# A two-layer diffusion backbone: a new plan for where the expert groups go in, and the unit ends on ScalarE's queue

## The reference, cut to what matters

```python
hl = modulate(rmsnorm(xl, norm1_g[l]), ...)           # norm1
out_c, out_l = token_mixers(hc, hl, w_in[l], ...)     # attention (da), mLSTM (ml), short convolution; merge
xl = xl + g1 * out_l
hl = modulate(rmsnorm(xl, norm2_g[l]), ...)
xl = xl + g2 * peer(hl, wq, keys, u_tab, v_tab)       # experts
```

## The kernel before

| stage | segment 1 | segment 2 | segment 5 |
|---|---|---|---|
| first route (pair 1) | 42, of which 22 at its last step | - | 40, of which 20 at its last step |
| swap | 2 | 2 | - |
| q | 3 | 4 | 3 |
| da, its 8 steps + 1 | 6 + 1 | 12 + 1 | 10 + 1 |
| ml_on (2 steps) | - | 5 | 4 |
| mc (8 steps) | 12 | 14 | 12 |
| mln (1 step) | 1 | 2 | 1 |
| merge (30 steps) | 35 | 40 | 33 |
| last route (8 steps) | 42 | 48 | 40 |

## Time and profile before

### The profile page before, as it was taken

How to read it: one execution, slowest core, us unless ns; L and a number is a source line. 1 busy time by engine, 2 the same in 40 slices (tenths; PEclk the granted TensorE clock), 3 DMA queues, 4 the chain that set the end, 5 groups by cost and what they waited for, 6 DMA issues and landing times.

```text
span 6141.9 us, 65028 instructions
## 1 busy us (share of the span) xinstructions
PE 3690.8 (60%) x22376; PEld 2569.9 (42%) x22376; DVE 2908.5 (47%) x6866; ACT 1680.3 (27%) x4742; POOL 1387.8 (23%) x1297
## 2 busy tenths in 40 slices
PE   4888786337774357774445566878545787433333
PEld 2677575215552235553223344767422565211111
DVE  0212324745447754446745444331575444764444
ACT  0111201214432242442233222210123343222222
POOL 0000000232222222232333333000122222223433
PEclk7798687658886677887666687759766788665555
DMA  7333034798998888998889998204578799789998
GB/s 285 137 129 126 1 110 168 302 351 337 359 380 313 312 315 317 350 408 313 336 350 386 369 404 369 100 1 146 195 289 339 278 376 387 308 307 379 405 410 361
DMA packets 331978, 1767.03 MB, mean 288 GB/s; under 512 B 96672, under 2 KB 109824, under 8 KB 140416
## 3 DMA queue, kind: packets, MB, share of 16 engines
q0 software_dynamic: 184320, 1342.26, 54.8%
q1 hardware_dynamic: 139648, 399.64, 17.9%
q10 hardware_dynamic: 7680, 20.98, 1.2%
HBM read 1737.95 MB, written 24.68 MB: 287 GB/s over the span
## 4 chain that ended last, share of the span: by engine, by line
PE 35%; DMA 26%; DVE 16%; ACT 5%; DVEq 4%; issue 4%; POOL 2%; ACTq 2%; SPq 0%; PEld 0%; PEldq 0%; POOLq 0%
PE psum L474 24%; DMA arena<-in_uv,arena 22%; PE psum L825 5%; DVE arena L2135 5%; POOL arena L1187 2%; DVE arena L2037 1%; DVE arena L2030 1%; DVE arena L2031 1%; PE psum L434 1%; DMA arena<-in_w_mix 1%; DVEq L2137 1%; DMA arena<-in_norm_g 1%; PE psum L655 1%; DMA arena<-x_rows 1%; PE psum L656 1%
## 5 line engine op out<-in xcount | busy, mean ns | idle before, releaser
L1187 POOL DMA_INDIRECT arena<-in_uv,arena x1280 | 1383.5, 1081 | 4719.6 <-PE psum L825 2741.5
L2135 DVE CUSTOM_DVE_ANT_0 arena<-arena 128x1024 f32<-128x1024 f32 x1280 | 1554.4, 1227 | 1418.7 <-DMA arena<-in_uv,arena 1329.5
L474 PE MATMUL psum<-arena 128*128 128x256 f32 (+2 forms) x8608 | 2041.3, 397 | 144.4 <-DVEq L1571 53.5
L825 PE MATMUL psum<-arena 128*32 128x256 f32 x10240 | 988.2, 523 | 1719.7 <-ACTq L1552 1657.3
L474 PEld LDWEIGHTS psum<-arena 128*128 128x128 f32 (+1 forms) x8608 | 1696.0, 203 | 514.3 <-issue 92.7
L825 PEld LDWEIGHTS psum<-arena 128*32 128x32 f32 x10240 | 335.1, 137 | 2288.9 <-ACTq L1552 1855.7
L1544 ACT ACTIVATE arena<-arena 128x2 f32<-128x2 f32 x640 | 131.1, 205 | 1879.6 <-DVEq L2137 1652.4
L1551 ACT ACTIVATE arena<-arena 128x32 f32<-128x32 f32 x1280 | 341.8, 314 | 45.6 <-issue 1.4
L434 PE MATMUL psum<-arena 128*128 128x128 f32 (+1 forms) x680 | 136.3, 361 | 340.5 <-DVE arena L1630 78.7
L1548 ACT ACTIVATE arena<-arena 128x1 f32<-128x1 f32 x1280 | 307.8, 287 | 46.7 <-issue 2.6
L434 PEld LDWEIGHTS psum<-arena 128*128 128x128 f32 (+1 forms) x680 | 105.2, 188 | 382.5 <-issue 191.7
(11 more groups left out here) (210 smaller groups left out, 2829.5 us busy)
## 6 DMA issues: line engine op xcount, KB each, us to landing
arena<-in_w_in SPq DMA_DIRECT2D x116, 1024.0 KB, 6.8
arena<-in_w_mix SPq DMA_DIRECT2D x120, 768.0 KB, 8.4
arena<-in_w_ada SPq DMA_DIRECT2D x32, 1536.0 KB, 16.2
arena<-in_w_wq SPq DMA_DIRECT2D x40, 1152.0 KB, 5.3
arena<-in_w_wo SPq DMA_DIRECT2D x20, 1024.0 KB, 9.2
arena<-h_rows ACTq DMA_DIRECT2D x160, 128.0 KB, 7.4
arena<-in_uv,arena POOLq DMA_INDIRECT x1280, 12.5
arena<-ada_rows SPq DMA_DIRECT2D x15, 512.0 KB, 8.0
```

The source lines that it names most:

```text
L474: ins = mm(out, a, b, start=(i == 0), stop=(i == last))
L825: ins = mm(acc_bank(u)[32 * q:32 * q + 32, gg * 256:gg * 256 + 256], DIAG[:, c, :], RING[:, sl, D + q * 256:D + (q + 1) * 256], start=(h, ...
L1187: pool.indirect_dma_start(RING[:, sl, :], None, io["uv"], bass.IndirectOffsetOnAxis(PICKED_U[b][:, h_, tg, a:a + 1], 0)).then_inc(gathered ...
L2135: V_.tensor_tensor_reduce(out=RING[:, sl, 0:D], in0=RING[:, sl, 0:D], in1=XT[:, gg, :], scale=1.0, scalar=0.0, op0=ALU.mult, op1=ALU.add, ...
```

## The change

Three edits. **The costs** in `steps()` are replaced: no longer microseconds of a step but roughly the number of groups that go beside it. **The sharing out** in `quotas()` gives a step the fraction cost/left of the places still to be given, so that places held back by `routed_upto` are spread over the steps after it; and segments 1 and 5 get 12 places more (`more` 16 to 28), segment 3 and the tail 12 fewer. **The unit ends**: SP's `group` is empty; the loads of G2P and XP and the stores of XP are issued by ACT, one place later in the walk than before, the stores after ACT has waited for `added`.

The plan after:

| stage | segment 1 | segment 2 | segment 5 |
|---|---|---|---|
| first route (pair 1) | 27, of which 7 at its last step | - | 26, of which 6 at its last step |
| swap | 1 | 1 | - |
| q | 3 | 2 | 2 |
| da, its 8 steps + 1 | 18 + 5 | 24 + 4 | 25 + 4 |
| ml_on | - | 12 | 12 |
| mc | 9 | 8 | 8 |
| mln | 10 | 8 | 8 |
| merge | 29 | 24 | 25 |
| last route | 54 | 45 | 46 |

Segment 3: norm1 14, kv 6, mlp 11, ml 23, norm1 14, qkv 9, mlp 16, mc 11 (four empty). In the last route of segments 1, 2 and 5 `routed_upto` now holds some places back too: the last steps of segment 2 and 5 are 5, 4, 8.

```diff
@@ -86,26 +86,26 @@
 
     n = len(pairs)
     if kind == "norm1":
-        return [4.0] * (2 * n)
+        return [5.0] * (2 * n)
     if kind in ("qkv", "kv", "q"):
-        return [2.5 if op[0] == "turn" else 7.0 for op in qkv_ops(kind) for p in pairs]
+        return [0.9 if op[0] == "turn" else 0.7 for op in qkv_ops(kind) for p in pairs]
     if kind == "da":
-        return [6.0 if u[2] > CT else 3.0 for u in da_units(l, pairs)] + [5.0] * n
+        return [3.1 if u[2] > CT else 2.0 for u in da_units(l, pairs)] + [4.0] * n
     if kind == "mlp":
-        return [1.0] * n + [3.5] * (len(ml_blocks(l, pairs)) * n) + [7.0] * (2 * n) + [6.0]
+        return [0.7] * n + [0.8] * (len(ml_blocks(l, pairs)) * n) + [1.0] * (2 * n) + [2.0]
     if kind in ("ml", "ml_back", "ml_on"):
-        return [10.0] * len(ml_units(kind, l, pairs))
+        return [6.0 if u[5] else 4.0 for u in ml_units(kind, l, pairs)]
     if kind == "mc":
-        return [7.0] * (2 * n) + [7.0] * (6 * n)
+        return [1.0] * (8 * n)
     if kind == "edge":
-        return [6.0] * 4
+        return [0.9] * 4
     if kind == "mln":
-        return [5.0] * n
+        return [8.0] * n
     if kind == "merge":
-        return [5.2] * 24 + [7.0] * 4 + [4.0] * 2
+        return [0.74] * 24 + [1.0] * 4 + [1.6] * 2
     if kind == "route":
-        return [24.0] * PH
-    return [8.0]
+        return [5.8] * PH
+    return [1.0]
 
 
 UNITS = [(0, t, f) for t in (2, 3, 0, 1, 4, 5) for f in range(2)] + [(1, t, f) for t in range(CT, NT) for f in range(2)]
@@ -136,7 +136,7 @@
     c = [("swap", 0, (2,))] + second_pair(0)
     c2 = [(k, 1, (0,)) for k in ("norm1", "kv", "mlp", "ml")] + ahead
     e1 = [("route", 1, (1,))] + second_pair(1)
-    tile, more = 2 * GROUPS, 16
+    tile, more = 2 * GROUPS, 28
     p0, p1 = sequence(range(0, 12)), sequence(range(12, 20))
     b_end, c_end, e_end = 2 * tile + more, 4 * tile + more, 2 * tile + more
     return [(a, [], 0), (b, p0[:b_end], 0), (c, p0[b_end:c_end], 0), (c2, p0[c_end:], 0), (first_pair(1), [], 0), (e1, p1[:e_end], 0),
@@ -162,15 +162,16 @@
 
     out = []
     for stages, items, lead in SEGMENTS:
-        total = sum(sum(steps(*st)) for st in stages)
-        done, cum, rows = lead, 0.0, []
+        left = sum(sum(steps(*st)) for st in stages)
+        done, aim, rows = lead, float(lead), []
         for st in stages:
             row = []
             for n, cost in enumerate(steps(*st)):
-                cum += cost
-                want = lead + int(round((len(items) - lead) * cum / total))
+                aim += (len(items) - aim) * min(1.0, cost / left)
+                left = max(left - cost, 1e-6)
                 if st[0] == "route" and n < PH - 1:
-                    want = max(done, min(want, routed_upto(items, st[1], st[2], n - 1)))
+                    aim = min(aim, float(routed_upto(items, st[1], st[2], n - 1)))
+                want = max(done, int(round(aim)))
                 row.append(want - done)
                 done = want
             rows.append(row)
@@ -398,6 +399,10 @@
 
             _, t, f = UNITS[u]
             return route_of(u) % 2, h, 4 * (t % 2) + 2 * f + gg
+
+        def ada_row(l, p, j):
+            st = 0 if p == 0 else 1
+            return ada_rows[2 * l + 1 - st:2 * l + 2 - st, j * D:(j + 1) * D]
 
         def last_unit(l, t):
             return UNITS.index((l, t, 1))
@@ -1028,10 +1033,6 @@
                     yield
                 barrier()
 
-            def ada_row(l, p, j):
-                st = 0 if p == 0 else 1
-                return ada_rows[2 * l + 1 - st:2 * l + 2 - st, j * D:(j + 1) * D]
-
             def merge(kind, l, pairs):
                 (p,) = pairs
                 g1, xs, mods = buf(l, p, "G1", [D]), buf(l, p, "XS2", [2, D]), buf(l, p, "MT", [2, D])
@@ -1090,28 +1091,7 @@
                 barrier()
 
             def group(i):
-                item = PSEQ[i]
-                if item is not None:
-                    u, g = item
-                    l, t, f = UNITS[u]
-                    if g == 8:
-                        if new_stream(u):
-                            if u:
-                                sp.wait_ge(s("added"), u)
-                            row = ada_row(l, t // 2, 5)
-                            for q in range(4):
-                                for gg in range(2):
-                                    sp.dma_start(G2P[32 * q:32 * q + 32, gg * 256:gg * 256 + 256], row[:, q * 256:(q + 1) * 256].to_broadcast([32, 256])).then_inc(s("g2_in"), 16)
-                        if u >= 2:
-                            sp.wait_ge(s("x2_stored"), 64 * (u - 1))
-                        for q in range(4):
-                            sp.dma_start(XP[32 * q:32 * q + 32, u % 2].rearrange("p (g n) -> p g n", g=2), x_of(u, q)).then_inc(s("xp_in"), 16)
-                tail = PSEQ[i - LAG_TAIL] if i >= LAG_TAIL else None
-                if tail is not None and tail[1] == GROUPS - 1:
-                    u = tail[0]
-                    sp.wait_ge(s("added"), u + 1)
-                    for q in range(4):
-                        sp.dma_start(x_of(u, q), XP[32 * q:32 * q + 32, u % 2].rearrange("p (g n) -> p g n", g=2)).then_inc(s("x2_stored"), 16)
+                return
 
             def swap(kind, l, pairs):
 
@@ -1527,10 +1507,30 @@
                             if ahead[0]:
                                 act.wait_ge(s("dots"), GROUPS * ahead[0])
                             load_xt(ahead[0], gg)
+                tail = PSEQ[i - LAG_TAIL - 1] if i > LAG_TAIL else None
+                if tail is not None and tail[1] == GROUPS - 1:
+                    u = tail[0]
+                    act.wait_ge(s("added"), u + 1)
+                    for q in range(4):
+                        act.dma_start(x_of(u, q), XP[32 * q:32 * q + 32, u % 2].rearrange("p (g n) -> p g n", g=2)).then_inc(s("x2_stored"), 16)
                 item = PSEQ[i - LAG_ACT] if i >= LAG_ACT else None
                 if item is None:
                     return
                 u, g = item
+                if g == 8:
+                    l, t, f = UNITS[u]
+                    if new_stream(u):
+                        act.wait_ge(s("ada_stored"), 64 * (l + 1))
+                        if u:
+                            act.wait_ge(s("added"), u)
+                        row = ada_row(l, t // 2, 5)
+                        for q in range(4):
+                            for gg in range(2):
+                                act.dma_start(G2P[32 * q:32 * q + 32, gg * 256:gg * 256 + 256], row[:, q * 256:(q + 1) * 256].to_broadcast([32, 256])).then_inc(s("g2_in"), 16)
+                    if u >= 2:
+                        act.wait_ge(s("x2_stored"), 64 * (u - 1))
+                    for q in range(4):
+                        act.dma_start(XP[32 * q:32 * q + 32, u % 2].rearrange("p (g n) -> p g n", g=2), x_of(u, q)).then_inc(s("xp_in"), 16)
                 if g % HG == 0:
                     act.wait_ge(s("picked"), picked_by(u, g // HG))
                 act.wait_ge(s("dots"), nxt("dots"))
```

## The result

| us | before | changed |
|---|---|---|
| median of 4 runs each (lowest, highest) | 6143.33 (6133.4, 6151.22) | 6235.57 (6229.0, 6240.95) |
| the profiled execution, its span | 6144.2, 6141.9 | 6230.4, 6228.2 |

The ratio of changed to before is 1.0151, 95% interval 1.0131 to 1.017. The change makes the kernel 92 us slower. The forecast was 6119, faster, with a range that ended at 6170.

What follows compares the result with a forecast made beforehand. The prediction took time as bytes at 405 GB/s plus idle of the DMA queues, no engine being the limit. Its terms, -49 - 4 - 10 + 18 + 12 - 4 + 12 = -25, took 6144.2 to 6119 us, range 6050 to 6170.

Steps and rivals of the forecast that it cites:

- What bounds the kernel: Whole kernel: time is bytes at 405 GB/s plus queue idle; a group moved to where queues idle can cost under 5.2 us.
- da, -49: da of segments 1, 2, 5: three-place steps take 16.5 us, queue idle falls from 71 to 22 us, saving 49.
- Rival C: da steps stay bound by gathers landing, 18.5 us each; da gives back the 49, kernel 6168 us; chance 0.18.
- Long chains, -4: ml_on, mln, norm1: gathers don't refill during the long chain; 2 us off for each of ml_on and norm1, -4.
- B: Ring also refills during chains of ml_on, mln and norm1, removing half their idle; kernel 6059 us; chance 0.14.
- Held-up groups, -10: First routes of segments 1 and 5: 29 held-up groups move out, saving 0.6 us each, 17 computed, 10 booked.
- Thinner steps, +18: merge, mc, q, kv, qkv lose groups and come down to PE's pace, so queues idle more: +18 us.
- Routes, +12: Last routes: groups added cost 5.2 us each, saved elsewhere; picks hold back the last steps, about 4 us a route, +12.
- The places moved between segments, 0: 12 + 12 places moved into segments 1 and 5 cost 5.2 us each and save as much elsewhere: 0.
- Unit ends, -4 and +12: Unit ends: SP freed of issues and waits gains 4 us; ACT's added issues and waits in its chains cost 12.
- Rival D: ACT's issues and wait lie on the path at each of 20 unit ends, 98 us; kernel 6205 us; chance 0.09.
- Rival E: A wash: thin merges, mc and late picks give back what da wins; kernel 6140 to 6150 us; chance 0.09.

Runs made afterwards that it cites:

- run 3: The changed kernel with the cost of a latent da step 2.0 instead of 3.1, so about two places a step: 6173.9 us, ratio 1.005.
- run 5: The kernel before with 12 places of segment 2 and 15 of segment 5 moved from merge to da: 6208.17 us, ratio 1.011.
- run 7: The changed kernel with PE one place late instead of two in da only: 6164.42 us, ratio 1.0038.
- Run 6: The kernel before with the new way of sharing out alone; costs, segment sizes and unit ends as before: 6102.99 us, ratio 0.9937.
- run 1: The changed kernel with the unit ends back on SP: 6245.55 us, ratio 1.0172.
- run 11: The changed kernel with segments 1 and 5 at their old length (`more` 16 instead of 28): 6234.2 us, ratio 1.0141.
- run 2: The kernel before with its old plan, only the unit ends moved to ACT: 6140.77 us, ratio 0.9995.
- run 9: The kernel before with the new way of sharing out and the unit ends on ACT: 6106.22 us, ratio 0.9937.
- run 8: Old costs except da's (three places a step), new sharing out and segment lengths, ends on ACT, PE one place late in da: 6124.58 us, ratio 0.9963.

## Why the prediction was wrong

**What bounds the kernel.** Held: the time is bytes at full rate and idle of the queues, though 405 GB/s is not the most that they do: the mlp stages of the changed kernel move 417 and 416 GB/s at 11 and 16 places (net -4.2 and -7.8, which the sum did not have). What failed is the next step, the sentence that a group moved to where the queues idle can cost less. Whether it does depends on why they idle. In da they idled because slots came free late, a latency, and more groups in a step only met that latency more often.

**da, -49: the step that failed.** The prediction took 16.5 us for a step of three places, just above the larger of an engine sum (16.2) and a queue sum (15.6). Both sums are those of work that overlaps. The step runs in series instead: measured 21.5 us (172.0 / 8) and 22.4 (179.5 / 8). Segment 1, with 2.25 places a step, takes 110.2, not 100. The missed term is the landing of the third group, issued inside its own step. Runs 3, 5 and 7 show it from three sides: without the third place 62 of the 92 us go; the third place put into the old kernel makes it anew; one place less of lag takes 25 and 20 us off segments 2 and 5. The evidence was in hand: the prediction noted that slots come free two places late and that the dots waited 2.68 us, and it knew the landing's 5.5 to 25.9 us. It did not count how many groups can be ahead (four less two) against three in a step.

**Rival C named this, and was undersized.** It had the mechanism (slots freed two places late, in the next step's groups) and a threshold of 17.5 us a step. But it priced the step at 18.5 and the loss at 49, to reach 6168; the step cost 21.5 to 22.4 and da came out 89 us above the forecast. It weighed the landing against the queues' pace (10.4 against 12.5 us) where it should have added it to the dense chain of 7.2 us and the groups' own 3.0 each. The "against" that it gave, that landings were long because of the load, did not help: in the trace the third group, first of its burst after POOL had stood 11.4 us, still took 5.5 us from issue to its first dot and 7.7 to its second.

**Long chains, -4: measured +13.9.** That they don't refill was right, and B is out: ml_on took 92.1 and 93.2 us, near the 90 forecast, and idled (1 - 292 / 405) x 92.1 = 26. ml_on and norm1 came out 7 us worse each, over two stages of either kind, where 2 were taken off. ml_on has six places at each step and norm1 seven, and DVE's waits for gathers grew: from none to 23.9 us in ml_on of segment 2, and from 7.0 to 42.1 in the first norm1 of segment 3. The row for ml_on in the changed kernel:

```profile
DVE arena L2135 <- DMA arena<-in_uv,arena: 23.9, 15, 4.9
```

No run changed these stages alone, so that the landings are the cause here is argued, not shown.

**Held-up groups, -10: measured -16.1.** Right in sign, nearer to the 17 computed than to the 10 booked. The stage is shorter by 85.3 (352.0 to 266.7), 80 forecast. Run 6 shows what this edit is worth without the new costs: -41 us, of which the first routes have 11 net; the rest stands in later stages.

**Thinner steps, +18: measured +42.** merge of segment 2 took 216.6 us at clock 0.93, with 48 gathers, against 200 to 215 forecast. The price was 203 from PE's sum; PE was busy 188.6, so the loss is in waits. The first 24 steps took 148 us, 147 forecast; the last six took 68 where 56 were forecast. The largest wait, from the answer on PE's waits in this stretch:

```profile
PE psum L439 <- DVE arena L2021: 19.9, 2, 18.8
```

This is at the stage's end. The same wait in the gather-free merge of segment 0, from which the prediction took its 48 us for the last six steps, is shorter (the kernel before):

```profile
PE psum L434 <- DVE arena L2021: 12.6, 2, 12.0
```

So this wait grew by 7 us beside gathers, more than half of the 13.6 us between 216.6 and 203. DVE's own waits tell most of why: before its part at L2014 it waits for the row of norm gains, a DMA that SP issues. First segment 0 of the kernel before, then the merge of segment 2 of the changed one:

```profile
DVE arena L2014 <- DMA arena<-in_norm_g: 6.6, 1, 6.6
DVE arena L2014 <- DMA arena<-in_norm_g: 11.8, 1, 11.8
```

And the stage's very end waits for the landing of the last group's gathers (4.25 and 2.27 us before its dots on DVE), so that PE stands for 5.93 us until the barrier. In segment 5 the wait for the row of gains is 6.1 us and PE's 14.7, so there it explains at most 2 us of a merge that is net +8.6. Run 5 shows the other half of the term: with 18 places the merge was at PE's pace and the queues at 336 GB/s. The idea, cover gone and PE setting the pace, was right; its size was not. In q, qkv and mc only the sums are known, not the wait behind them; mlp, 12 net below its places, was not in the forecast's list.

**Routes, +12: measured +7.2**, 380.1, 343.1 and 334.3 us for 54, 45 and 46 places: near in sum, and in part by luck. By segment it is -2.1, +11.7 and -2.5, not 4 each, and the same route of segment 2 takes 331.6 us in run 1. **The places moved between segments, 0**: right, run 11.

**Unit ends, -4 and +12.** Both are wrong in the old plan (runs 2 and 9: 0), and their sum of +8 is not seen in the new one either (run 1: between 0 and -10). Rival D is out. Rival E was half right: thin stages do cost, but da wins nothing for them to give back.

The sum of the forecast was therefore off by +89 in da, +24 in thin stages and +18 in chains, and by less than 10 in each other line. The range failed for the same reason: its top came from C's 18.5, which was an estimate of a rate and not the length of a chain.

What stays open is why the mixed plan (run 8) lost 22 us to run 6 although its da is better (the stages are known, last routes, mc, da's end and q, and not the reason); why places spread thinly by run 6 come so cheap; and whether da could reach 16 us a step with a deeper ring, which was not tried.

## What to carry to other kernels

Before filling a stage whose queues idle, count how many transfers can be ahead of the consumer: ring depth less the places by which slots are released late (here 4 less 2). In this kernel more per step than that put one landing in series with the step, and the price was the chain's length, not the larger of two rates. Test the edits of a change apart: here the way of sharing out was worth -41 us, and the cost table that came with it +128 (run 11's 6234.2 less run 9's 6106.22; the two kernels differ in the cost table alone).

## What the runs showed that was not expected

A group's gathers are slow to come even right after a pause of POOL: issued at 2317.15 and 2318.39, they let the dots start at 2322.69 and 2326.13, 5.5 and 7.7 us later. A release one place earlier for PE was worth 71 us in da alone and cost 429 us when used everywhere (6664.94 against 6235.57); 283 of them are in the merges, where PE then waits for ACT in most groups (77.0 us over 20 waits in that of segment 2). And 192 DMA issues put on ACT (0.45 us each at the median in the changed kernel, so by estimate 86 us) cost nothing that could be measured (ratio 0.9995).
